# Inversion products of two heads as one 128x128 product, in a two-layer-plus-retention kernel

## The chip, the cores and the metric

The kernel runs on one core of one Trainium2 chip. The metric is the device time of one execution in microseconds (us). Of the kernel before, three runs gave 2006.71 us as their median (2004.17 to 2009.91). All rows are of one profiled execution of 2008.5 us.

## The reference

The model works on 512 tokens of width 1024: an RWKV-7 layer with its MLP, a sliding-window attention layer with its MLP, and a retention and Fourier block with a gated convolutional feed-forward. The part that matters here is the recurrence of the RWKV-7 layer, 16 heads of 64 channels, in float32:

```python
def wkv7(r, w, k, v, a, b):
    def step(S, inp):
        r_t, w_t, k_t, v_t, a_t, b_t = inp
        sa = jnp.einsum('bhvk,bhk->bhv', S, a_t)
        S = S * w_t[:, :, None, :] + sa[..., None] * b_t[:, :, None, :] + v_t[..., None] * k_t[:, :, None, :]
        y = jnp.einsum('bhvk,bhk->bhv', S, r_t)
        return S, y
```

The kernel computes it in chunks of 64 tokens. Inside a chunk the corrections `sa` of the 64 steps depend on each other through a strictly triangular 64x64 matrix per head; the kernel inverts identity minus that matrix.

## The kernel before, in words

**Layout.** Channels lie on the 128 partitions in 8 blocks (CB = 8), so a block holds two heads: head 0 on partitions 0 to 63, head 1 on 64 to 127. There are 8 chunks (NCH) of 64 tokens (HC), taken in 4 groups of two; x is the chunk within its group, g the group.

**The inversion.** It goes by five levels (LEVELS = 5). At each level the triangular matrix LL is masked so that only that level's blocks stay (LM, on GpSimd, `level_mask`, L2922), and two products follow: `inverse_left` (L2294) multiplies the masked matrix with the inverse so far, Z, which lies in the right half of the tile GBZ; ScalarE copies the result out of PSUM (QS, L914); `inverse_right` (L2302) multiplies the transposed inverse TI with QS; VectorE adds the result to Z (`inverse_sum`, L1474) and transposes Z for the next level (`turned`, L1468, one instruction over 128 partitions). Each product is made per block and per head: a 64x64 stationary matrix on 64 partitions, 64 moving columns, 8 blocks x 2 heads = 16 matmuls in the code. In float32 each becomes two weight loads and two matmuls in the profile, so 32 of each.

**The other products.** Score products feed the recurrence: `score_wide` (L2265, 128 moving columns; four blocks per job) and `score_narrow` (L2274 and L2276, 64 columns, eight blocks per job). They read one head's partitions and write the other head's (`cross`), so they use the two 64x64 quarters of the array that the inversion products of the same two heads don't. VectorE masks the wide ones (`score_mask`, L1460), ScalarE copies the narrow ones (L903). The recurrence itself is made of `correction` (L2381), `values_sum` (L2351), `output_states` (L2340), `solved` (L2363) and `off` (L2322 to L2331).

**The order.** It is written out by hand as beats. Beat b issues on TensorE: the left product of (g, level, x) = `inverse_at(b)` with the wide job of that beat between its matmuls; the right product of the beat before with the narrow job of this beat between its matmuls; then the recurrence's products for units of earlier beats; and in the first eight beats a `bonus` product (L2253, two matmuls of 512 columns on 32x128 tiles). A group has 10 beats (5 levels x 2 chunks), the four groups 40; about ten beats of recurrence alone follow. A table says which of the ten beats of a group have a wide job (8) and which a narrow one (8); the last group has fewer. Six score jobs run ahead of the first beat. Each engine has its own copy of the beat loop and waits on semaphores of the others: the left product for `lm` (GpSimd) and for the sum of its last level, the right one for QS and TI. LM has two tiles per x, so GpSimd may run two levels ahead. The stage is unrolled: each of its instructions is in the program once.

Of the kernel before, what the change touches and what calls it, by code (L numbers as in the profile page):

```python
# [16 lines left out]
ALU = mybir.AluOpType  # L17
# [3 lines left out]
P = 128  # L21
C = 1024
CB = C // P
# [14 lines left out]
LEVELS = 5  # L38
HC = 64
# [24 lines left out]
SQ_AT = {n: i for i, n in enumerate(SQUARES)}  # L64
# [115 lines left out]
def program(nc, t, out, book):  # L180
    ctx = ExitStack()
    with ctx:
# [3 lines left out]
        def at(name, kb, shape, dt=F32):  # L186
            return nc.alloc_sbuf_tensor_at(name, [P] + list(shape), dt, offset=base + int(kb * KB))
# [5 lines left out]
        sqs = at("sqs", 2, [N_SQ * P])  # L193
# [22 lines left out]
        PB = [ctx.enter_context(nc.psum_tensor(f"bank{i}", [P, 512], F32)) for i in range(8)]  # L216
# [4 lines left out]
        STEP = {}  # L221
# [31 lines left out]
        def phase_done(who):  # L253

            phases[who] += 1
            return 4 * phases[who]
# [105 lines left out]
        def masked_bank(beat):  # L362

            return (2, 7)[sorted(MASKED).index(beat % PER) % 2]
# [20 lines left out]
        GBZ = [at(f"GBZ{n}", kb, [CB, P]) for n, kb in enumerate((32, 40, 192, 196, 16, 24))]  # L385
        GKM = [at(f"GKM{n}", 20 + 8 * n, [CB, P]) for n in range(4)]
        LL = [at(f"LL{n}", 48 + 2 * n, [CB, HC]) for n in range(4)]
        VT = [at(f"VT{n}", 56 + 2 * n, [CB, HD]) for n in range(4)]
        LM = [[at(f"LM{x}{n}", 64 + 4 * x + 2 * n, [CB, HC]) for n in range(2)] for x in range(2)]
        QS = [at(f"QS{x}", 72 + 2 * x, [CB, HC]) for x in range(2)]  # L390
        TI = [at(f"TI{x}", 76 + 2 * x, [CB, HC]) for x in range(2)]
        SM = [at(f"SM{x}", 80 + 2 * x, [CB, HD]) for x in range(2)]
        WB = [at(f"WB{n}", 200 + 0.5 * n, [P]) for n in range(2)]
        DIAG = [at(f"DIAG{n}", 201 + 1.5 * n, [3 * P]) for n in range(2)]
# [132 lines left out]
        def half_of(name, n):  # L527

            return sq(name)[:, n * HC:(n + 1) * HC]

        def every(ap):

            return ap.unsqueeze(1).to_broadcast([P, CB, HC])

        def level(lv):

            return every(half_of(("lvl01", "lvl23", "lvl4id")[lv // 2], lv % 2))

        def pairs(ap):
            return ap.rearrange("p (a b) -> p a b", a=CB)  # L540
# [11 lines left out]
        def twice(ap):  # L552
            return ap.rearrange("p (a b) -> p a b", a=2)
# [25 lines left out]
        def tok(j):  # L579
            return slice(j * HC, (j + 1) * HC)  # L580

        def head(h):
            return slice(HD * h, HD * h + HD)
# [699 lines left out]
        def _(dve):  # L1283
# [92 lines left out]
            ds, di, dr, dg = (STEP["dve_" + n] for n in ("score", "inv", "rec", "gn"))  # L1376
# [68 lines left out]
            dve.tensor_copy(RKS[:], PB[4][:]).then_inc(dp.sem, dp.step())  # L1445
            dve.drain().then_inc(phase, 1)
            dve.wait_ge(phase, phase_done("dve"))
            dve.memset(SM[0][:], 0.0).then_inc(dr.sem, dr.step("m0"))
            ps, pi = STEP["pe_score"], STEP["pe_inv"]

            def bonus(cb):
# [10 lines left out]
            def turned(g, lv, x):  # L1462

                if lv == 0:
                    dve.wait_ge(STEP["pool_score"].sem, STEP["pool_score"].at(("z0", 2 * g + x)))
                else:
                    dve.wait_ge(di.sem, di.at(("z", g, lv - 1, x)))
                dve.transpose(TI[x][:], GBZ[(2 * g + x) % 6][:, :, HC:P]).then_inc(di.sem, di.step(("t", g, lv, x)))  # L1468

            def inverse_sum(g, lv, x):  # L1470

# [42 lines left out]
            for beat in range(BEATS):  # L1514
                z, m, w, y = inverse_at(beat - 1), job_at(MASKED, beat), recurrence_at(beat), recurrence_at(beat - 2)
# [6 lines left out]
                if z:  # L1522
                    g, lv, x = z
# [534 lines left out]
        def _(pe):  # L2058
# [51 lines left out]
            for kb in range(CB):  # L2110
                if kb == 4:
                    idle_work(6, PB[4])
                g = kb % 4
# [4 lines left out]
            for tb in range(TB):  # L2118
                mm = pe.matmul(PB[5][:, tb:tb + 1], PARTS[:, chunk(tb)], sq("ones")[:, 0:1], start=True, stop=True)
# [5 lines left out]
            for kb in range(CB):  # L2125
                pe.wait_ge(dl.sem, dl.at(("x", kb)))
                pe.matmul(PB[0][:], lg1[:, kb, 0:P], xl[kb][:], start=kb == 0, stop=kb == CB - 1)
                if kb % 4 == 3:
                    for g in range(4):
                        mm = pe.matmul(PB[1][32 * g:32 * g + 32, :], lg1[:, kb - 3 + g, P:LORA_G], xl[kb - 3 + g][:], start=kb == 3, stop=kb == CB - 1)  # L2130
# [4 lines left out]
            for kb in range(CB):  # L2135
                n = CB + 2 * kb
# [4 lines left out]
            for kb in range(CB):  # L2141
                pe.wait_ge(al.sem, al.at(("csq", kb)))
                g = kb % 4
# [15 lines left out]
            for q in range(3 * CB):  # L2159
                m, o = q % CB, PB[4 + q % 4][:]  # L2160
# [8 lines left out]
                if q < CB:  # L2169
# [3 lines left out]
                    mm = pe.matmul(o, low2["ga"][2][:, chunk(m)], hid2["ga"][1][:], start=False, stop=True)  # L2173
                elif q < 2 * CB:
                    mm = three(o, pieces(hid2["w"], chunk(m // 2)), pieces(low2["w"], slice(m % 2 * 512, m % 2 * 512 + 512)))
                else:
                    mm = three(o, pieces(low2["a"], chunk(m)), pieces(hid2["a"], every_token))
# [64 lines left out]
            din, ain, drc, arc = STEP["dve_inv"], STEP["act_inv"], STEP["dve_rec"], STEP["act_rec"]  # L2242
# [17 lines left out]
            def score_wide(j, job, bank, a):  # L2260

                cb = a + 4 * (job % 3)
                for h in range(2):
                    hs = head(h)
                    mm = pe.matmul(PB[bank][cross(h), chunk(a)], (BT if job < 2 else KT)[hs, cb, tok(j)], RA[hs, :, cb, tok(j)], start=True, stop=True)  # L2265
                if a == 3:
                    mm.then_inc(ps.sem, ps.step((j, job)))
# [21 lines left out]

            def inverse_left(g, lv, x, cb):  # L2290

                for h in range(2):
                    hs = head(h)
                    mm = pe.matmul(PB[x][hs, tok(cb)], LM[x][(LEVELS * g + lv) % 2][hs, cb, :], GBZ[(2 * g + x) % 6][hs, cb, HC:P], start=True, stop=True)  # L2294
                if cb == CB - 1:
                    mm.then_inc(pi.sem, pi.step(("q", g, lv, x)))

            def inverse_right(g, lv, x, cb):

                for h in range(2):  # L2300
                    hs = head(h)
                    mm = pe.matmul(PB[x][hs, tok(cb)], TI[x][hs, cb, :], QS[x][hs, cb, :], start=True, stop=True)  # L2302
                if cb == CB - 1:
                    mm.then_inc(pi.sem, pi.step(("z", g, lv, x)))

# [89 lines left out]
            for beat in range(BEATS):  # L2395
                q, z = inverse_at(beat), inverse_at(beat - 1)
                m, c = job_at(MASKED, beat), job_at(COPIED, beat)
                w, u, y, w2 = (recurrence_at(beat - ago) for ago in (0, 1, 2, -1))
                if q:
                    inverse_left_ready(*q)  # L2400
                if m:
                    score_free(MASKED, beat)
                for n in range(CB):
                    if q:
                        inverse_left(*q, n)
                    if m and n % 2 == 0:
                        score_wide(*m, masked_bank(beat), n // 2)
                if z:
                    pe.wait_ge(ain.sem, ain.at(("q", *z)))
                    pe.wait_ge(din.sem, din.at(("t", *z)))  # L2410
                if c:
                    score_free(COPIED, beat)
                for n in range(CB):
                    if z:
                        inverse_right(*z, n)
                    if c:
                        score_narrow(*c, 3, n)
                if y is not None:
                    off_ready(y)
                if w2 == 0:  # L2420
                    pe.wait_ge(dp.sem, dp.at(("bonus", CB - 1)))
                elif u is not None or w2 is not None:
                    pe.wait_ge(arc.sem, arc.at(("diag", beat - 1)))
                for n in range(CB):
                    if y is not None:
                        off(y, n)
                    if n in (0, 1) and w2 is not None:
                        mm = values_sum(w2, n)
                        if n == 1 and u is None:
                            mm.then_inc(pr.sem, pr.step(("diag", beat)))  # L2430
                    if n in (2, 3) and u is not None:
                        output_states(u, n - 2)
                    if n in (4, 6) and u is not None:
                        mm = solved(u, n // 2 - 2)
                        if n == 6:
                            mm.then_inc(pr.sem, pr.step(("diag", beat)))
                if w is not None:
                    correction(w)
                if beat < CB:
                    bonus(beat)  # L2440
                if beat == VSUM_AT:
                    early_sums()
# [401 lines left out]
            h = RH - 1  # L2844
# [45 lines left out]
        def _(pool):  # L2890
# [24 lines left out]
            def level_mask(g, lv, x):  # L2915

                j, at_level = 2 * g + x, LEVELS * g + lv
                if lv == 0:
                    pool.wait_ge(STEP["act_tok"].sem, STEP["act_tok"].at((j, 2)))
                if at_level >= 2:  # L2920
                    pool.wait_ge(STEP["pe_inv"].sem, STEP["pe_inv"].at(("q", (at_level - 2) // LEVELS, (at_level - 2) % LEVELS, x)))
                pool.tensor_tensor(LM[x][at_level % 2][:], LL[j % 4][:], level(lv), ALU.mult).then_inc(pc.sem, pc.step(("lm", j, lv)))  # L2922

            def scaled(j):

# [130 lines left out]
```

## Time and profile before

| what | value |
|---|---|
| median of 3 runs | 2006.71 us |
| profiled execution, its own time | 2008.5 us |
| its span, first to last instruction | 2006.6 us |
| TensorE busy | 1906.9 us (95%) |
| VectorE, ScalarE, GpSimd busy | 57%, 38%, 11% |
| the 40 beats with inversion products | 221.26 to 390.60 us |
| TensorE busy in them | 127.05 of 169.34 us |

A busy time is the union of an engine's records, so matmuls that overlap in different parts of the array count once. PE is TensorE's matmuls, PEld its weight loads, DVE VectorE, ACT ScalarE, POOL GpSimd. "Issue" is idle time for which the profile shows nothing that was waited for.

### The profile page before, as it was taken

The numbers are of one execution on the slowest core, as the hardware profiler recorded it, in microseconds if no ns is written. First come the engines' busy times: TensorE is split into PE (matmuls) and PEld (weight loads), VectorE is DVE, ScalarE is ACT, GpSimd is POOL, SyncE is SP. The second block draws the span as 40 slices with busy tenths as digits, with TensorE's granted clock in tenths as the row PEclk, the third lists the DMA queues.
The fourth block names the chain that finished last, engine by engine and source line by source line (L and its number), as shares of the span: only waits on it lengthen the run. The fifth ranks groups of instructions, "written<-read, shape, count | busy, mean of one in ns | idle before, by whom it ended". The sixth has DMA issues, their size and how long they took to land.

```text
span 2006.6 us, 34728 instructions
## 1 busy us (share of the span) xinstructions
PE 1906.9 (95%) x14308; PEld 1532.7 (76%) x14308; DVE 1139.9 (57%) x1749; ACT 771.7 (38%) x1255; POOL 221.6 (11%) x178
## 2 busy tenths in 40 slices
PE   7999966789999999998999999999999999999997
PEld 3877766667788787765778787877888788888885
DVE  6789755474444434567484746576554366566323
ACT  6777333334232212447532222235243244444211
POOL 1000344200201202014110202020000010000001
PEclk9999999999999999999999999999999989999999
DMA  5420000232332232220344454535520222322421
GB/s 196 139 84 32 3 4 4 84 131 95 93 96 92 77 114 79 98 69 33 126 147 159 148 180 143 208 126 169 156 77 32 74 84 90 110 94 84 152 89 42
DMA packets 61000, 201.44 MB, mean 100 GB/s; under 512 B 8000, under 2 KB 11200, under 8 KB 59584
## 3 DMA queue, kind: packets, MB, share of 16 engines
q1 hardware_dynamic: 60096, 192.93, 28.9%
q10 hardware_dynamic: 768, 6.55, 1.0%
q8 instruction: 103, 1.69, 0.4%
q14 instruction: 33, 0.27, 0.0%
HBM read 190.68 MB, written 6.42 MB: 98 GB/s over the span
## 4 chain that ended last, share of the span: by engine, by line
PE 70%; issue 19%; DVE 6%; POOL 2%; ACT 2%; DMA 0%; DVEq 0%; POOLq 0%; SPq 0%; ACTq 0%
PE bank L2097 17%; PE bank L2099 17%; PE bank L2098 17%; POOL HS L2958 2%; PE bank L2294 2%; PE bank L2302 1%; DVE HR L1682 1%; DVE wlo L1292 1%; PE bank L2265 1%; PE bank L2618 1%; PE bank L2604 1%; PE bank L2781 1%; DVE ADS L1668 1%; PE bank L2638 1%; PE bank L2104 1%
## 5 line engine op out<-in xcount | busy, mean ns | idle before, releaser
L1292 DVE TENSOR_TENSOR wlo<-raw,whi 128x1024 fp32r<-128x1024 f32 x270 | 327.4, 1223 | 568.9 <-ACT whi L741 567.7
L741 ACT ACTIVATE whi<-raw 128x1024 fp32r<-128x1024 f32 x270 | 282.2, 1057 | 708.5 <-PE bank L2099 691.9
L2097 PE MATMUL bank<-inh,whi 128*128 128x512 f32 x1200 | 470.8, 392 | 1.9 <-DVE inl L1559 1.6
L2099 PE MATMUL bank<-inh,wlo 128*128 128x512 f32 x1200 | 467.1, 389 | 0.0
L2098 PE MATMUL bank<-inl,whi 128*128 128x512 f32 x1200 | 467.0, 389 | 0.0
L2097 PEld LDWEIGHTS bank<-inh,whi 128*128 128x128 f32 x1200 | 225.3, 188 | 58.4 <-issue 6.6
L2099 PEld LDWEIGHTS bank<-inh,wlo 128*128 128x128 f32 x1200 | 225.2, 188 | 47.0
L2098 PEld LDWEIGHTS bank<-inl,whi 128*128 128x128 f32 x1200 | 225.3, 188 | 46.7 <-issue 0.7
L2097 PE MATMUL bank<-hidh,whi 128*128 128x512 f32 x576 | 228.6, 397 | 8.2 <-DVE HR L1682 5.4
L2099 PE MATMUL bank<-hidh,wlo 128*128 128x512 f32 x576 | 224.5, 390 | 0.0
L2098 PE MATMUL bank<-hidl,whi 128*128 128x512 f32 x576 | 224.3, 389 | 0.0
L2958 POOL TENSOR_TENSOR HS<-HR 128x512 f32<-128x512 f32 x64 | 85.8, 1374 | 678.1 <-DVE HR L1682 678.1
L2097 PEld LDWEIGHTS bank<-hidh,whi 128*128 128x128 f32 x576 | 108.1, 188 | 41.3 <-DVE HR L1682 14.7
L2099 PEld LDWEIGHTS bank<-hidh,wlo 128*128 128x128 f32 x576 | 108.1, 188 | 22.9
L2098 PEld LDWEIGHTS bank<-hidl,whi 128*128 128x128 f32 x576 | 108.2, 188 | 20.9
L2097 PE MATMUL bank<-xmh,whi 128*128 128x512 f32 x192 | 76.5, 398 | 0.0
L2098 PE MATMUL bank<-xml,whi 128*128 128x512 f32 x192 | 74.8, 389 | 0.0
L2099 PE MATMUL bank<-xmh,wlo 128*128 128x512 f32 x192 | 74.8, 389 | 0.0
L1668 DVE SCALAR_TENSOR_TENSOR ADS<-ADW,LT,ADS 128x1536 f32<-128x1536 f32 (+1 forms) x56 | 69.0, 1279 | 0.0
L2097 PE MATMUL bank<-GH,whi 128*128 128x512 f32 x176 | 68.6, 390 | 0.0
L2099 PE MATMUL bank<-GH,wlo 128*128 128x512 f32 x176 | 68.5, 389 | 0.0
L2098 PE MATMUL bank<-GL,whi 128*128 128x512 f32 x176 | 68.5, 389 | 0.0
(423 smaller groups left out, 2818.4 us busy)
## 6 DMA issues: line engine op xcount, KB each, us to landing
raw<-in_mlp_w SPq DMA_DIRECT2D x128, 512.0 KB, 3.6
ADW<-in_w_ada SPq DMA_DIRECT2D x32, 768.0 KB, 5.0
raw<-in_w_up SPq DMA_DIRECT2D x44, 512.0 KB, 3.5
raw<-in_w_in SPq DMA_DIRECT2D x28, 512.0 KB, 3.6
raw<-in_a_w_rkv SPq DMA_DIRECT2D x24, 512.0 KB, 3.4
raw<-in_w_down SPq DMA_DIRECT2D x22, 512.0 KB, 3.4
raw<-in_a_wo SPq DMA_DIRECT2D x8, 512.0 KB, 7.7
raw<-in_b_wq SPq DMA_DIRECT2D x8, 512.0 KB, 3.3
```

Source lines behind the costliest of these rows:

```text
L741: act.activation(whi[u % SLOTS][:, :], raw[u % SLOTS][:, :], ACT.Copy).then_inc(w_hi, 1)
L1292: dve.tensor_tensor(lo[:, :], r[:, :], h[:, :].bitcast(F32), ALU.subtract).then_inc(w_lo, 1)
L1668: dve.scalar_tensor_tensor(acc, w, c_, acc, ALU.mult, ALU.add).then_inc(dmo.sem, dmo.step(("sum", tag, v, k), ("sum", tag, k)))
L1682: dve.scalar_tensor_tensor(HR[m % 4][:], PB[m][:], 0.0, RS[:], ALU.max, ALU.mult).then_inc(dmlp.sem, dmlp.step(("r", nm, m)))
L2097: pe.matmul(o, w[:, wc], xh, start=start, stop=False)
L2098: pe.matmul(o, w[:, wc], xl_, start=False, stop=False)
L2099: return pe.matmul(o, r[:, wc], xh, start=False, stop=stop)
L2104: pe.matmul(o, xh, w[:, wc], start=start, stop=False)
L2265: mm = pe.matmul(PB[bank][cross(h), chunk(a)], (BT if job < 2 else KT)[hs, cb, tok(j)], RA[hs, :, cb, tok(j)], start=True, stop=True)
L2294: mm = pe.matmul(PB[x][hs, tok(cb)], LM[x][(LEVELS * g + lv) % 2][hs, cb, :], GBZ[(2 * g + x) % 6][hs, cb, HC:P], start=True, stop=True)
L2302: mm = pe.matmul(PB[x][hs, tok(cb)], TI[x][hs, cb, :], QS[x][hs, cb, :], start=True, stop=True)
L2958: pool.tensor_tensor(HS[m % 4][:], HR[m % 4][:], HR[m % 4][:], ALU.mult).then_inc(STEP["pool_mlp"].sem, STEP["pool_mlp"].step(("hs", nm, m)))
```

## The change

Both heads of a block go into one product. The stationary operands become 128x128 block-diagonal matrices, head 0's 64x64 matrix top left, head 1's bottom right, zero elsewhere: LM and TI get 128 columns per block. The level masks are laid out the same way in a new tile LVL (five levels x 128 columns), so that the mask product also writes LM's zeros: it reads LL twice over and writes 1024 elements per partition instead of 512. TI's zero halves are set once, and the transpose writes each head's diagonal block in an instruction of its own. The products' moving operands (Z and QS) and their results stay where they were. The wide and the narrow score jobs leave the loops of the inversion products and get loops of their own behind them.

```diff
-        LM = [[at(f"LM{x}{n}", 64 + 4 * x + 2 * n, [CB, HC]) for n in range(2)] for x in range(2)]
+        LM = [[at(f"LM{x}{n}", 64 + 20 * x + 4 * n, [CB, P]) for n in range(2)] for x in range(2)]
+        LVL = at("LVL", 204, [LEVELS, P])
-        TI = [at(f"TI{x}", 76 + 2 * x, [CB, HC]) for x in range(2)]
+        TI = [at(f"TI{x}", 76 + 16 * x, [CB, P]) for x in range(2)]
...
+            for x in range(2):
+                for h in range(2):
+                    dve.memset(TI[x][head(h), :, tok(1 - h)], 0.0).then_inc(dr.sem, dr.step(("zero", x)))
+            dve.memset(LVL[:], 0.0).then_inc(dr.sem, dr.step("zero levels"))
             dve.memset(SM[0][:], 0.0).then_inc(dr.sem, dr.step("m0"))
+            dve.wait_ge(dr.sem, dr.at("zero levels"))
+            for h in range(2):
+                masks = sqs[head(h), SQ_AT["lvl01"] * P:SQ_AT["lvl01"] * P + LEVELS * HC]
+                dve.tensor_copy(LVL[head(h), :, tok(h)], masks.rearrange("p (a b) -> p a b", a=LEVELS)).then_inc(dr.sem, dr.step("levels"))
...
-                dve.transpose(TI[x][:], GBZ[(2 * g + x) % 6][:, :, HC:P]).then_inc(di.sem, di.step(("t", g, lv, x)))
+                for h in range(2):
+                    dve.transpose(TI[x][head(h), :, tok(h)], GBZ[(2 * g + x) % 6][head(h), :, HC:P]).then_inc(di.sem, di.step(("t", g, lv, x)))
...
-                for h in range(2):
-                    hs = head(h)
-                    mm = pe.matmul(PB[x][hs, tok(cb)], LM[x][(LEVELS * g + lv) % 2][hs, cb, :], GBZ[(2 * g + x) % 6][hs, cb, HC:P], start=True, stop=True)
+                mm = pe.matmul(PB[x][:, tok(cb)], LM[x][(LEVELS * g + lv) % 2][:, cb, :], GBZ[(2 * g + x) % 6][:, cb, HC:P], start=True, stop=True)
...
-                for h in range(2):
-                    hs = head(h)
-                    mm = pe.matmul(PB[x][hs, tok(cb)], TI[x][hs, cb, :], QS[x][hs, cb, :], start=True, stop=True)
+                mm = pe.matmul(PB[x][:, tok(cb)], TI[x][:, cb, :], QS[x][:, cb, :], start=True, stop=True)
...
                 for n in range(CB):
                     if q:
                         inverse_left(*q, n)
-                    if m and n % 2 == 0:
-                        score_wide(*m, masked_bank(beat), n // 2)
+                for n in range(CB // 2):
+                    if m:
+                        score_wide(*m, masked_bank(beat), n)
...
                 for n in range(CB):
                     if z:
                         inverse_right(*z, n)
+                for n in range(CB):
                     if c:
                         score_narrow(*c, 3, n)
...
+                if at_level == x == 0:
+                    pool.wait_ge(STEP["dve_rec"].sem, STEP["dve_rec"].at("levels"))
...
-                pool.tensor_tensor(LM[x][at_level % 2][:], LL[j % 4][:], level(lv), ALU.mult).then_inc(pc.sem, pc.step(("lm", j, lv)))
+                pool.tensor_tensor(LM[x][at_level % 2][:].rearrange("p c (a b) -> p c a b", a=2), LL[j % 4][:].unsqueeze(2).to_broadcast([P, CB, 2, HC]),
+                                   twice(LVL[:, lv, :]).unsqueeze(1).to_broadcast([P, CB, 2, HC]), ALU.mult).then_inc(pc.sem, pc.step(("lm", j, lv)))
```

## Rows read from the trace of the kernel before

**Rows 1.** The page, TensorE's line: busy us (share of the span) xinstructions.

```profile
PE 1906.9 (95%) x14308; PEld 1532.7 (76%) x14308; DVE 1139.9 (57%) x1749; ACT 771.7 (38%) x1255; POOL 221.6 (11%) x178
```

**Rows 2.** Busy time by stretch, its columns in the first line.

```profile
core 0: us, PE busy (x) PEld busy (x) DVE busy (x) ACT busy (x) POOL busy (x), PEclk, DMA share, GB/s
221.26:390.60 169.34, 127.05 (x5539) 112.80 (x5536) 97.00 (x211) 55.43 (x107) 71.89 (x60) 1.00 0.02 4
225.00:247.00 22.00, 22.00 (x724) 16.05 (x718) 17.31 (x27) 7.16 (x12) 12.24 (x12) 1.00 0.01 4
264.81:268.39 3.58, 2.47 (x127) 2.33 (x127) 1.36 (x6) 0.60 (x1) 1.27 (x1) 1.00 0.02 5
```

**Rows 3.** Chain of waits, 221.26 to 390.60 us, shares by line.

```profile
by line: issue 24.0%; PE bank L2294 18.5%; PE bank L2302 17.2%; PE bank L2265 8.3%; PE bank L2276 6.0%; PE bank L2253 5.0%; PE bank L2331 2.6%; PE bank L2381 2.5%; PE bank L2324 2.3%; PE bank L2363 2.2%; PE bank L2329 2.1%; PE bank L2322 2.
```

**Rows 4.** TensorE's waits, same stretch: who waited for what, us, times, longest.

```profile
PE bank L2294 <- DVE GBZ L1474: 2.8, 4, 0.7
```

**Rows 5.** DMA queues, same stretch: packets, MB, share of 16 engines.

```profile
q8 instruction: 44, 0.72, 1.9%
```

**Rows 6.** Groups by line, 218 to 400 us: busy us, mean ns | idle before.

```profile
L2294 PE MATMUL bank<-GBZ,LM 64*64 64x64 f32 x1280 | 50.0, 222 | 12.8 <-issue 8.8 <-DVE GBZ L1474 2.8 <-POOL LM L2922 0.8
L2302 PE MATMUL bank<-QS,TI 64*64 64x64 f32 x1280 | 47.3, 219 | 4.8 <-issue 4.6
```

**Rows 7.** Timeline of TensorE ahead of the first beat: start us, us, instruction.

```profile
218.57 1.92 PE L2265 MATMUL bank<-RA,AA 64*64 64x128 f32 x32
220.32 1.10 PE L2274 MATMUL bank<-AA,RA 64*64 64x64 f32 x32
221.26 0.27 PE L2294 MATMUL bank<-GBZ,LM 64*64 64x64 f32 x2
```

**Rows 8.** Timeline of TensorE over the fifth beat.

```profile
233.47 0.27 PE L2294 MATMUL bank<-GBZ,LM 64*64 64x64 f32 x2
...
234.40 0.22 PE L2276 MATMUL bank<-sqs,AA 64*64 64x64 f32 x2
...
235.32 0.22 PE L2302 MATMUL bank<-QS,TI 64*64 64x64 f32 x2
235.48 1.12 PE L2253 MATMUL bank<-RKS,heads 32*128 32x512 f32 x2
236.53 0.27 PE L2294 MATMUL bank<-GBZ,LM 64*64 64x64 f32 x2
```

**Rows 9.** Timeline of weight loads: two unbroken runs of 128x128 products elsewhere.

```profile
1399.61 3.65 PEld L2695 LDWEIGHTS bank<-VC,KW 128*128 128x128 f32 x32 [0.91 <-ACT VC L1134]
...
1606.43 0.97 PEld L2840 LDWEIGHTS bank<-sqs,PARTS 128*128 128x128 f32 x8 [1.66 <-DVE MX L1995]
```

**Rows 10.** Groups by line and shape, weight loads.

```profile
L2294 PEld LDWEIGHTS bank<-GBZ,LM 64*64 64x64 f32 x1280 | 42.9, 134 | 23.5 <-issue 16.8 <-POOL LM L2922 5.6 <-POOL RA L2929 0.8
...
L2695 PEld LDWEIGHTS bank<-VC,KW 128*128 128x128 f32 x32 | 3.6, 192 | 0.9 <-ACT VC L1134 0.9
```

**Rows 11.** Groups by line and shape, VectorE and GpSimd.

```profile
L1468 DVE STREAM_TRANSPOSE TI<-GBZ 128x512 f32<-128x512 f32 x40 | 28.4, 710 | 1.1
...
L1310 DVE MEMSET hid<- 64x512 f32 x1 | 0.5, 485 | 0.0
L1448 DVE MEMSET SM<- 128x512 f32 x1 | 0.5, 485 | 0.3 <-DVEq L1446 0.3
...
L2922 POOL TENSOR_TENSOR LM<-LL,sqs 128x512 f32<-128x512 f32 x40 | 50.3, 1274 | 28.6 <-PE bank L2294 28.6
L2929 POOL TENSOR_TENSOR RA<-RA,FS 128x512 f32<-128x512 f32 x14 | 14.5, 1058 | 32.3 <-DVE GKM L1460 32.3
...
L2903 POOL TENSOR_TENSOR lw_lo<-lw,lw_hi 128x1024 fp32r<-128x1024 f32 x1 | 2.4, 2425 | 14.9 <-DVE gb_xh L1335 14.9
```

**Rows 12.** Timeline of VectorE and GpSimd at the start of the stage.

```profile
216.98 0.69 DVE L1460 TENSOR_TENSOR GBZ<-bank,sqs 128x512 f32<-128x512 f32 x1 [0.48 <-PE bank L2265]
...
218.71 1.26 POOL L2913 TENSOR_TENSOR GBZ<-GBZ,sqs 128x512 f32<-128x512 f32 x1 [167.12 <-DVE GBZ L1460]
219.94 1.27 POOL L2922 TENSOR_TENSOR LM<-LL,sqs 128x512 f32<-128x512 f32 x1
```

More of the change, by code:

```diff
@@ L533, in every @@
             return ap.unsqueeze(1).to_broadcast([P, CB, HC])
-        def level(lv):
-            return every(half_of(("lvl01", "lvl23", "lvl4id")[lv // 2], lv % 2))
         def pairs(ap):
@@ L2410, in _ @@
                     pe.wait_ge(din.sem, din.at(("t", *z)))
+                    if z[:2] == (0, 0):
+                        pe.wait_ge(drc.sem, drc.at(("zero", z[2])))
                 if c:
```

## The prediction

> **What bounds the kernel now.** Four views, in this order. The page first: TensorE is busy for 95% of the span [rows 1], so what a stage costs on TensorE goes straight into the time, unless TensorE idles there. The change touches one stage only, the chunked recurrence, whose 40 beats with an inversion product run from 221.26 to 390.60 us. The table by stretch [rows 2] says that TensorE does idle there: 127.05 us busy of 169.34, with the granted clock at 1.00 (the 2.4 GHz level). The chain of waits of the same stretch [rows 3] says for what: 24.0% of it, 40.6 us, is "issue", time in which TensorE waits for no other engine; the waits for others are small (the largest, for the sum of VectorE, is 2.8 us, [rows 4]). The DMA view names it [rows 5]: the instruction queue fetched 44 times in that stretch, 0.72 MB, so 16 KB each. At 64 bytes an instruction (my reading of 16 KB against the 5539 matmuls and 5536 weight loads of [rows 2]: 11075/44 = 252) that is one fetch per block of some 254 matmuls and loads, and one fetch every 169.34/44 = 3.85 us. The third line of [rows 2] is one such block: 127 + 127 instructions, 3.58 us, 2.47 of it busy.
>
> Is 3.85 us a floor for a block, or a pause added to each? From 225 to 247 us [rows 2] TensorE runs 1442 of them in 22.00 us without idling, 3.9 us for 254: work that takes as long as the fetch shows no pause. So I read a floor. A block costs the larger of 3.85 us and its own work; today's work is 127.05/44 = 2.9 us.
>
> **The change, part by part.** (All terms are us, against the profiled execution, 2008.5 us with a span of 2006.6; the median shown is 2006.7, 1.8 below it.)
>
> 1. *Instructions removed.* Each product had 32 matmuls and 32 loads (16 products of 64x64, each in two instructions), 1280 + 1280 matmuls over 40 products of each kind [rows 6]. They become 16 + 16 each. 2560 of 11075 instructions go, so 33.8 fetches stay: the floor falls from 169 to 130.
>
> 2. *What a product costs.* Today 32 matmuls take 0.93 (L2294 from 233.47 until L2276 starts at 234.40, [rows 8]), 29 ns each. That is the rate of two tiles, rows 0-63 to columns 0-63 and rows 64-127 to 64-127, working side by side. The new ones take the whole array. A load of 128 columns instead of 64 has a record of 192 ns instead of 134 [rows 10], and in unbroken runs 128x128 instructions in f32 follow each other at (3.65 - 0.19)/31 = 0.112 with 128 moving columns and at (0.97 - 0.19)/7 = 0.111 with one [rows 9]. Our 64 moving columns lie between these, so 0.112: 16 x 0.112 = 1.79 a product. Added: 1.79 - 0.93 = 0.86, over 80 products 68.8. Nothing hides it: from 225 to 247 TensorE is busy all the time, and later each block has only the fetch pause as cover, which is counted in step 5. Bounds from the rows: 0.058, one tile's pace today (two tiles at 29 ns), which adds 0; and 0.192, the load's whole record with no overlap, which adds 80 x (3.07 - 0.93) = 171. The runs of [rows 9] have the new shape, so I take theirs and give the ends little.
>
> 3. *The covered products come out.* Score products write "across" (rows of one head to the columns of the other), so they used the two tiles that the inversion left free. The beat at 233.47 shows it [rows 8]: left product and 16 wide matmuls together end by 234.40, right product and 32 narrow ones together by 235.35. Alone, 32 wide ones take 220.32 - 218.57 = 1.75 and 32 narrow ones 221.26 - 220.32 = 0.94 [rows 7]. A whole-array matmul leaves no tile free, and the change puts both kinds in loops of their own. Wide jobs in these beats: 28 (8 a group in three groups, 4 in the last), each 16 matmuls, 0.875: 24.5, less the 0.05 by which they stretched the left section: 23.1. Narrow jobs: 30 at 0.94: 28.2. Together 51.3. Bounds: 0 if they still overlapped something, which the whole array excludes but for the edges; 51.3 is at the upper end.
>
> 4. *Changing tiles.* Before L2253, which uses 32x128 tiles, the next start, 235.48, comes 0.14 after the last L2302 (a pair at 235.32 and 235.34) instead of 0.03: 0.11 to 0.12 extra; behind it L2294 starts at 236.53, when two of 0.53 are through, so nothing [rows 8]. Two entries a beat into 128x128: 80 x 0.12 = 9.6. Bounds: 0, and 0.22 (one matmul's own record, [rows 6]) at each of 160 changes, 35.
> The Trainium skill ("TensorEngine Tiling (Array Packing)", Key Properties) says that changing the tiling mode, not just the tile, drains the engine. The change makes four mode changes a beat where the later beats now have none. By the rule every one of the 160 would cost a drain, and the rows show one side of a pair only; the time that it gives is rival B below.
>
> 5. *The pauses go.* Work after: 127.05 + 68.8 + 51.3 + 9.6 = 256.8 over 33.8 blocks is 7.6 a block, twice the floor of 3.85. A block spans about one beat and always holds some 30 whole-array matmuls (3.6 alone), so no block falls under the floor. All 42.3 of idle time but the 1.7 that is no issue goes: 258.5 against 169.3, +89.2.
>
> 6. *VectorE.* The transpose [rows 11] is now one per head, on 64 partitions. A memset of 64x512 takes 485 ns, as much as one of 128x512, so halving partitions saves nothing: 40 more of 0.71 (0.64 apart), 28 in all. They come behind the sum for which the next left product waits, and the right product that reads them comes a beat later, so beats of 6 cover them; in today's beats it would be up to 26. Cost 0.
>
> 7. *GpSimd.* A mask product doubles to 1024 elements: from 1.27 to about 2.42, as the 128x1024 row shows [rows 11]. Ten beats hold 10 of these, two additions of 1.26 and four scalings of 1.06: 31. The ten beats take 10 x 6.5 = 65. Hidden; its cover ends at beats of 3.1.
>
> 8. *Start.* VectorE zeroes four half tiles (4 x 0.485) and the level tile (0.6, scaled from the same row) and copies the levels twice (each taken as nearly one memset of [rows 11], 0.9 together) before its first score mask: 3.5, of which 0.5 was idle there [rows 12]. GpSimd's first addition then starts 3.0 later and its first level mask [rows 12] takes 1.15 longer; the first left product waits for just these: +4. Bounds 2 and 5.
>
> Sum: 89.2 + 4 = 93. 2008.5 + 93 = 2101.5 for a profiled execution, 2100 as a median.
>
> **The rivals.**
> A, *the other side: supply of instructions decides.* If a 128x128 product took no longer than a 64x64 pair and the score products still ran beside it, work would stay at 127 under the new floor of 130: 130 - 169 + 4 = -35, 1972. For it: the 24% of [rows 3] and one fetch per 3.85. Against: the 0.112 of [rows 9]. It decides from the point where the work after stays below 169 - 4 = 165; already the uncovered scores alone (127 + 51 = 178) pass that, so both steps 2 and 3 must be wrong. 0.04.
> B, *each of the 160 changes of mode drains,* 0.22 each: 35 instead of 9.6, 2125. For it: the 0.12 of [rows 8] is for one side only, and small matmuls keep little in flight. Against: 64x64 after 32x128 cost nothing. 0.13.
> C, *the pause is added to every block.* Then 40.6/44 = 0.92 stays for each of 33.8 blocks, 31 more: 2131. Against: no idle time from 225 to 247. 0.08.
> D, *the work overlaps more than counted:* half of the 51.3 of step 3 stays covered, because loads of one mode slip under the matmuls of the other: 2074. Nothing in the rows shows it. 0.07.
> E, no change of more than 0.3% (6 us, about what a measurement of this kernel can tell from none): work would have to end at 165 by chance. 0.01.
>
> **The numbers.** Forecast 2100, chance 0.67, its own range 2085 to 2115 (the bounds of steps 2 and 8 and small waits). The range reaches over D and over B and C: 2068 to 2134; A and the far tails stay out, below 0.2. Slower by over 0.3%: 0.95; the same: 0.01; faster: 0.04.
>
> **What would show it.** In the profile after: L2294 and L2302's successors with 640 records each, 112 ns from start to start, 1.8 us a product (steps 1, 2); wide and narrow matmuls behind them, not between (step 3); a beat like the one at 233.47 at about 3.06 + 0.86 x 2 + 0.83 + 0.94 + 0.24 = 6.8; the stage some 259 long with "issue" near nothing and 33 or 34 fetches (step 5); GpSimd's mask at 2.4, and nobody waiting for it behind the first. All other stages as before. I am wrong if the 128x128 products follow each other at 60 ns or less, if TensorE still idles for a sixth of the stage (C), or if gaps of 0.2 stand at each change of mode (B).

## The result, and the profile after

The changed kernel takes 2130.93 us as a median of four runs (2101.66 to 2160.65) against 2006.66; the ratio is 1.057, with an interval of 1.046 to 1.068. The ratio leaves out the longest run, whose clock was lowest, and takes the mean of the other three; the medians alone give 1.062. On the two chips of e1 and e12 the ratio was 1.049 (1.041 to 1.057) and 1.064 (1.059 to 1.069). It is slower, as forecast. The profiled execution, 2101.66 us with a span of 2099.7, lies on the forecast for one (2101.5); the median lies 31 above 2100, near the upper end of the range (2134). Two questions, then: where 93 us come from in the profiled run, and why most runs take some 30 or 60 more.

The table by stretch: the stage of the 40 beats, then its first ten beats and the other thirty, after the change.

```profile
core 0: us, PE busy (x) PEld busy (x) DVE busy (x) ACT busy (x) POOL busy (x), PEclk, DMA share, GB/s
225.98:481.45 255.47, 255.47 (x4252) 237.32 (x4254) 127.45 (x249) 54.98 (x106) 113.95 (x60) 0.99 0.01 3
225.98:290.61 64.63, 64.63 (x712) 55.37 (x712) 30.18 (x44) 10.15 (x17) 29.84 (x16) 0.95 0.01 2
290.61:481.45 190.84, 190.84 (x3546) 181.95 (x3542) 97.28 (x206) 44.82 (x89) 84.11 (x45) 1.00 0.02 4
```

And the same two parts of the kernel before:

```profile
221.26:252.34 31.08, 29.45 (x1022) 22.32 (x1019) 23.56 (x36) 11.44 (x20) 17.95 (x15) 1.00 0.02 4
252.34:390.60 138.26, 97.59 (x4517) 90.48 (x4518) 73.45 (x176) 43.99 (x88) 53.93 (x46) 1.00 0.02 5
```

The stage went from 169.34 [rows 2] to 255.47 us, and TensorE, idle for a quarter of it before, is never idle now: 255.47 busy of 255.47, with a quarter fewer matmuls (4252 instead of 5539). The first ten beats grew by 33.5, the others by 52.6, the start came 4.7 later (225.98 instead of 221.26): 90.8 of the span's 93.1. The rest, 2.3, is outside the stage.

The chain of waits of the stage; "issue", 24.0% in [rows 3], is no longer among the first lines, and both products together are 60% instead of 36%.

```profile
by line: PE bank L2298 30.7%; PE bank L2304 29.5%; PE bank L2271 11.5%; PE bank L2282 10.0%; PE bank L2259 3.4%; PE bank L2280 2.5%; PE bank L2324 2.3%; PE bank L2383 2.1%; PE bank L2333 2.0%; PE bank L2331 2.0%; PE bank L2326 1.5%; PE bank
```

The DMA view, instruction fetches of the stage, 34 where [rows 5] has 44:

```profile
q8 instruction: 34, 0.56, 0.9%
```

The timeline of TensorE over the fifth beat, the one of [rows 8] (start us, us, instruction):

```profile
252.85 2.00 PE L2298 MATMUL bank<-GBZ,LM 128*128 128x64 f32 x16
254.78 1.09 PE L2271 MATMUL bank<-RA,AA 64*64 64x128 f32 x16
255.80 2.00 PE L2304 MATMUL bank<-QS,TI 128*128 128x64 f32 x16
257.73 1.15 PE L2282 MATMUL bank<-sqs,AA 64*64 64x64 f32 x32
258.81 1.12 PE L2259 MATMUL bank<-RKS,heads 32*128 32x512 f32 x2
259.86 0.32 PE L2298 MATMUL bank<-GBZ,LM 128*128 128x64 f32 x1
```

From start to start: left product (L2298) 1.93, wide job (L2271) 1.02, right product (L2304) 1.93, narrow job (L2282) 1.08, bonus (L2259) 1.05; in all 7.01 where it was 3.06. Before, the first two together took 0.93 and the next two 0.95.

### The profile page after: what moved, and what is told of

It is laid out like the page before. It is cut to its first block, busy times and chain, and to the rows that moved or that the text cites. A ratio compares the mean times of both kernels' runs of the same rounds, so it can differ in the third digit from the quotient of the medians.

```text
span 2099.7 us, 32217 instructions
## 1 busy us (share of the span) xinstructions
PE 2038.6 (97%) x13028; PEld 1658.8 (79%) x13028; DVE 1174.6 (56%) x1796; ACT 771.9 (37%) x1255; POOL 264.8 (13%) x178
## 4 chain that ended last, share of the span: by engine, by line
PE 73%; issue 16%; DVE 6%; POOL 2%; ACT 2%; DMA 0%; DVEq 0%; POOLq 0%; SPq 0%; ACTq 0%
PE bank L2103 17%; PE bank L2105 16%; PE bank L2104 16%; PE bank L2298 4%; PE bank L2304 4%; POOL HS L2967 2%; PE bank L2271 2%; PE bank L2282 1%; DVE HR L1688 1%; PE bank L2098 1%; PE bank L2624 1%; DVE wlo L1289 1%; PE bank L2610 1%; PE bank L2787 1%; DVE ADS L1674 1%
## 5 line engine op out<-in xcount | busy, mean ns | idle before, releaser
L2930 POOL TENSOR_TENSOR LM<-LL,LVL 128x1024 f32<-128x1024 f32 x40 | 93.6, 2354 | 37.8 <-PE bank L2298 37.8
L2298 PEld LDWEIGHTS bank<-GBZ,LM 128*128 128x128 f32 x640 | 75.5, 194 | 12.8 <-POOL LM L2930 5.4
L2298 PE MATMUL bank<-GBZ,LM 128*128 128x64 f32 x640 | 81.0, 280 | 4.3 <-POOL LM L2930 4.3
L2304 PE MATMUL bank<-QS,TI 128*128 128x64 f32 x640 | 79.4, 277 | 0.0
L2304 PEld LDWEIGHTS bank<-QS,TI 128*128 128x128 f32 x640 | 74.5, 192 | 4.7 <-issue 4.6
```

The lines of the kernel that those rows point to most:

```text
L2298: mm = pe.matmul(PB[x][:, tok(cb)], LM[x][(LEVELS * g + lv) % 2][:, cb, :], GBZ[(2 * g + x) % 6][:, cb, HC:P], start=True, stop=True)
L2304: mm = pe.matmul(PB[x][:, tok(cb)], TI[x][:, cb, :], QS[x][:, cb, :], start=True, stop=True)
L2930: pool.tensor_tensor(LM[x][at_level % 2][:].rearrange("p c (a b) -> p c a b", a=2), LL[j % 4][:].unsqueeze(2).to_broadcast([P, CB, 2, HC]) ...
```

## The experiments

Most change one thing of one of the two kernels; times are medians, and each time of the kernel before was taken on the same chip. Spans and beats are of the profiled runs. Estimates "by the line of spans and clocks" use 0.44 us of span for each us at half clock, a fit through the 14 runs of the changed kernel in the result, e1 and e12; the time at half clock is 2 x (1 - mean clock) x span.

**e1, the changed kernel again**, no edit.

> The changed kernel once more, to see its times beside their granted clocks, since its runs lay between 2101.66 and 2160.65 us while the profiled one gave 2101.66. Theory (work of TensorE, plus a clock that falls in some runs): times again spread over some tens of us, and each run's span follows from its clock: the four spans so far rise by 28.1, 59.0 and 30.5 us while the time at half clock, 2 x (1 - clock) x span, rises from 50 to 111, 177 and 119, so half a microsecond for each at 1.2 GHz. Rival (waits that fall differently from run to run, not the clock): spans that differ at one and the same clock.

2115.47 (2100.2 to 2132.3) against 2012.74. Its spans and mean clocks were 2098.2 at 0.990, 2103.3 at 0.986, 2123.8 at 0.975 and 2130.3 at 0.972, near the line that was expected (these four give 0.42 us for each us at half clock, the first four 0.46): the spread is the clock's. What the clock does, and where, e8 and e12 show.

**e2, the order alone.** In the kernel before:

```diff
                 for n in range(CB):
                     if q:
                         inverse_left(*q, n)
-                    if m and n % 2 == 0:
-                        score_wide(*m, masked_bank(beat), n // 2)
+                for n in range(CB // 2):
+                    if m:
+                        score_wide(*m, masked_bank(beat), n)
...
                     if z:
                         inverse_right(*z, n)
+                for n in range(CB):
                     if c:
                         score_narrow(*c, 3, n)
```

> The kernel before, with one thing of the change: wide and narrow score jobs come behind the inversion products in loops of their own; the products stay 64x64 per head. Step 3 of the prediction: work of the 40 beats rises from 127 by 51 to 178, while the instructions, so the floor of 3.85 us a fetch, stay (169). A late beat with everything has some 300 instructions (4.6 us by the floor) and 4.8 us of work, an early one is work alone (3.06 + 0.83 + 0.94): early ten beats +15, late ones +2 to +10. I expect 2020 to 2035 us. Rival (the supply of instructions alone decides): no change, 2007. Rival (a pause is added to every block whatever its work): +51, 2058.

2017.53 against 2012.74, ratio 1.0017 (1.0005 to 1.0029): 5 us where 13 to 28 were expected (2020 to 2035 on a kernel before of 2007). Work rose by 27.0 (37.03 + 117.04 against 127.05), not by the 51 counted. By stretch, first ten beats and the other thirty:

```profile
221.85:259.00 37.15, 37.03 (x1022) 30.18 (x1017) 23.26 (x36) 10.77 (x18) 17.53 (x15) 1.00 0.02 4
259.00:396.07 137.07, 117.04 (x4524) 111.77 (x4526) 73.57 (x176) 44.73 (x89) 54.42 (x46) 1.00 0.02 5
```

The thirty later beats hold 19.5 us more work (117.04 against 97.59) and take 1.2 less: the pauses are not added to the work but take it in, as the floor of the prediction has it, and "issue" falls from 24.0% to 11.6% of the stage's chain. The stage again had 44 fetches; that these are what sets the floor is read from their count and from "issue", and this run, which leaves their number alone, can't show it. The early beats, where little idled before (29.45 busy of 31.08), pay: +6.1. That is less than the 15 expected, because two jobs in different quarters of the array still overlap at their borders. The first wide matmuls start here before the last left ones, and the right product starts at 238.24, before the last wide ones (238.56), so this wide job adds some 0.3 to its beat and not 0.83:

```profile
236.97 0.97 PE L2294 MATMUL bank<-GBZ,LM 64*64 64x64 f32 x26
237.74 0.33 PE L2265 MATMUL bank<-RA,AA 64*64 64x128 f32 x2
237.78 0.28 PE L2294 MATMUL bank<-GBZ,LM 64*64 64x64 f32 x4
```

**e3, whole-array products with the score jobs between them**: the changed kernel with e2's edit taken back.

> The changed kernel with the score jobs back between the matmuls of the inversion products, as before. In the changed kernel's trace a change between whole-array and quarter matmuls costs 0.10 to 0.14 us from start to start. Here a beat with a wide job makes 8 such changes in its left part and one with a narrow job 16 in its right part. Theory (each change drains): 28 x 6 x 0.12 + 30 x 14 x 0.12 = +70 us over the changed kernel's 2102, so some 2170. Rival D of the prediction (loads of one mode slip under matmuls of the other, so covering would come back if the order were restored): 2050 to 2075.

2343.24, 1.16 of the kernel before, far over both theories. Its clock, 0.904 over the whole profiled run, is the larger part of it:

```profile
227.10:237.00 9.90, 9.86 (x66) 7.23 (x66) 2.01 (x3) 1.19 (x2) 9.90 (x5) 0.50 0.01 2
260.00:300.00 40.00, 40.00 (x187) 28.80 (x188) 9.74 (x14) 2.98 (x5) 8.26 (x4) 0.50 0.00 0
300.00:730.00 430.00, 428.77 (x3890) 344.73 (x3891) 111.53 (x226) 49.57 (x97) 92.87 (x50) 0.62 0.01 3
```

TensorE is busy nearly throughout, and most of the time at 1.2 GHz. An estimate parts the two: a mean clock of 0.904 over 2352.2 us makes 451 us at half clock, 401 more than in the changed kernel, which by the line of spans and clocks cost 177. Without them the span would be some 2176, 76 more than the changed kernel's, where the theory of costly changes had 70. So the old order would not have saved the score jobs' cover; with their separate 1.02 and 1.08 in the beat above, rival D is out.

**e4, everything but TensorE's part.** The changed kernel, score jobs between the products again, and the products per head on the diagonal halves:

```diff
-                mm = pe.matmul(PB[x][:, tok(cb)], TI[x][:, cb, :], QS[x][:, cb, :], start=True, stop=True)
+                for h in range(2):
+                    hs = head(h)
+                    mm = pe.matmul(PB[x][hs, tok(cb)], TI[x][hs, cb, tok(h)], QS[x][hs, cb, :], start=True, stop=True)
...
```

> Everything of the change but TensorE's part: GpSimd builds 128-column masks (2.35 us instead of 1.27), VectorE transposes per head and fills the tiles at the start, while TensorE keeps the 64x64 products with the score jobs between them, reading the diagonal halves. Steps 6 to 8: covered but for the start, +4: 2010 to 2013 us. Rival (VectorE or GpSimd becomes the bound once beats are short, as they are here at 4.1 us: ten masks and the rest take GpSimd 30 of 41): up to +26, 2033, with waits of TensorE for LM or GBZ.

2018.97 against 2012.74, +6.2 (ratio 1.0030, 1.0016 to 1.0043). In the profiled run the first left product comes 3.6 later (224.9 instead of 221.3), and the stage is 3.3 longer, 172.7. Of the wait for GpSimd's masks, 4.3 is that late start and only 3.0 lies in later beats:

```profile
PE bank L2300 <- POOL LM L2932: 7.3, 4, 4.3
```

What lengthens the stage is the clock of its first two beats, which end at 234.87 and take 9.96 where they took 6.08. The clock falls in the pause before the first product:

```profile
224.90:234.00 9.10, 9.10 (x195) 7.41 (x196) 3.46 (x6) 1.80 (x4) 9.10 (x5) 0.53 0.02 4
```

**e5 and e6, instructions that bring no work**, in either kernel:

```diff
                 if q:
+                    for _ in range(32):
+                        pe.wait_ge(in_tri, 16)
                     inverse_left_ready(*q)
```

> The kernel before with 32 more waits on TensorE at the head of each of the 40 beats, all on a semaphore that has long had its value: instructions that bring no work. Theory of a floor (3.85 us for a block of 256 instructions): 1280 more are 5 fetches, so +19 us in the late beats and in the early ones alike (these run just at the floor): 2028 to 2034 against the kernel before. Rival (TensorE's work and its waits for other engines bound the stage, fetches are incidental): within 4 us of the kernel before.

> The changed kernel with the same 32 waits a beat. Theory of a floor: a beat has some 230 instructions in 6.4 us, 262 with the waits, 3.9 us by the floor, so no change: 0 to +3 us against the changed kernel, stage 255 to 258. Rival (each instruction, or each fetch, costs its own time whatever the work): +19 here as well.

e5: 2031.29 against 2009.17, as the floor had it, but not for its reason: 46 fetches, not 49, and 20.5 us of waits for VectorE's transposes. e6: 2224.86, where 0 to 3 us over the changed kernel were expected. TensorE idled 32 of the stage's 365.6 us, at the heads of the beats:

```profile
PE bank L2298 <- issue: 19.0, 21, 1.4
PE bank L2298 <- POOL LM L2932: 9.7, 5, 4.6
PE bank L2298 <- DVE TI L1474: 7.4, 7, 1.4
```

The waits take time of their own, so this pair can't test the floor; I don't count it for it. What e6 did show is the clock: 0.70 from 300 to 592 us, while the kernel before idles more (42 us of 169) and stays at 1.00. By the line of spans and clocks that is 81 of its 112 us over the changed kernel (an estimate, from a mean clock of 0.947). The waits alone, with 64x64 products, take e5's stage to 0.94.

**e7, one of the two products.** Left products whole-array, wide jobs behind them; right products per head with the narrow jobs between, as in e4.

> Half of the change: left products whole-array with the wide jobs behind them, right products 64x64 per head with the narrow jobs between them. By the durations of the changed kernel (16 x 0.115 = 1.84 a product, wide jobs alone 0.88, 0.12 for each of two changes of mode a beat): work 127 + 40 x 0.9 + 23 + 10 = 196 against a floor of 150, so stage 196 to 202, +27 to +33, and +4 to +5 at the start: 2042 to 2052. If the whole-array products cost by a state of the engine that both kinds together bring about (the clock in the first place), this one keeps its clock and its runs lie within 5 us; if single whole-array runs are enough, its runs spread like the changed kernel's.

2036.46 against 2009.17: +27, below the 2042 to 2052 expected. The stage takes 188.8 where 196 to 202 were counted, 183.4 of it busy, "issue" 2.0% of its chain; its right products start before the wide job ahead of them has issued its last matmul (237.70 and 238.02 in the second beat), an overlap that was not counted. The first product uses up most of the 42 us of pause, so it costs 27 with its start; the second one then pays in full, some 65 more. The four runs lie between 2030.4 and 2040.7, clock 0.984 to 0.988: a spread of 10 us and not 5, but none on the lower levels, so in these four runs whole-array left products alone did not bring the long fall.

**e8, the fillings off the path**: GpSimd zeroes and fills LVL before its first addition, VectorE zeroes TI's halves among its first score masks and behind its first transpose.

> The changed kernel with the filling of the tiles off the path: GpSimd, idle until its first addition, zeroes and fills the level tile; VectorE zeroes the halves of TI in its gaps between the first score masks. The changed kernel started its first left product at 226.0 instead of 221.3 and ran that beat at half clock behind the pause (8.1 us for work of some 5.1). Theory: -4.5 for the start, less the 1.1 that the first mask costs more, and -3 if the clock does not fall: 5 to 7 us under the changed kernel (2092 to 2095 for a run of full clock). Rival (the fall of the clock has nothing to do with the pause): -3.5.

The first left product starts at 221.85, 4.1 earlier, and the first beat takes 4.93 instead of 8.09: for this the theory held. Yet the median is 2125.99, far over the 2092 to 2095 expected of a run of full clock, because its four runs all lost the clock for longer (means of 0.969 to 0.977); with that taken off by the line of spans and clocks, the profiled span of 2122.6 would be some 2096 (an estimate). This profile shows the loss. Busy time by stretch:

```profile
240.00:260.00 20.00, 20.00 (x210) 16.91 (x209) 10.90 (x17) 2.98 (x5) 8.27 (x4) 0.99 0.00 1
260.00:280.00 20.00, 20.00 (x137) 17.52 (x137) 6.01 (x9) 2.22 (x4) 4.38 (x3) 0.50 0.01 2
280.00:300.00 20.00, 20.00 (x124) 17.42 (x122) 4.17 (x6) 1.96 (x4) 1.08 (x1) 0.50 0.00 1
300.00:320.00 20.00, 20.00 (x174) 18.96 (x175) 5.01 (x8) 2.73 (x6) 10.72 (x6) 0.50 0.00 1
320.00:340.00 20.00, 20.00 (x330) 18.92 (x327) 9.18 (x19) 3.31 (x7) 7.86 (x5) 0.80 0.01 2
340.00:360.00 20.00, 20.00 (x393) 19.12 (x392) 10.71 (x25) 4.97 (x10) 5.94 (x3) 1.00 0.01 3
```

From about 260 to 328 us the granted clock is 0.50 (1.2 GHz), with TensorE busy in every microsecond from 240 on. It falls in the seventh beat, and it is back in the thirteenth.

**e9 and e11, an added product of 512 columns.** The changed kernel with one more product ahead of each left one:

```diff
+                if q:
+                    pe.matmul(PB[q[2]][:], sq("ones"), V[:, 0, :], start=True, stop=True)
                 for n in range(CB):
                     if q:
                         inverse_left(*q, n)
```

> The changed kernel with one more product ahead of each of the 40 left ones, 128x128 against 512 columns into the same bank, overwritten by the left product: two instructions of some 0.43 us in which the array streams columns without a load between. It adds 0.86 x 40 = 34 us of work. Theory (the clock falls because whole-array products of 64 columns spend half their time on loads, so the array does little though it is never idle): with the columns the clock stays at its upper level, all runs lie within 10 us of each other, near 2100 + 34 = 2134, clock 0.986 or more, and perhaps 3 lower since the first beat is not at half clock. Rival (the clock falls by the mode changes or by chance of the chip, whatever else streams): runs spread by 30 us and more as the changed kernel's did, 2134 to 2190.

> The kernel with the 512-column products ahead of the left ones once more, on the same chip as the changed kernel, for the clocks of more runs. So far one run in five had a mean clock under 0.98, of the changed kernel five in eight. Theory (streaming columns hold the clock): at most one or two of some six runs under 0.98, the rest at 2133 to 2139. Rival (it falls by chance whatever streams): three or more under 0.98.

e9: 2133.2, 2134.2, 2137.4, 2138.9, and one of 2195.9, where all five were expected within 10 us. e11, its profiled run among five: 2136.3 to 2139.0, clock 0.987 or 0.988. So 9 of 10 runs kept the clock and lie within 6 us, at the price of the added work.

**e12, the changed kernel beside e11.**

> The changed kernel once more beside it: more than half of its runs under a mean clock of 0.98, the spans again on the line of 0.47 us for each us at half clock: 2100 at 0.99 to 2160 at 0.96. Rival (the fall belongs to a chip or an hour, not to the kernel): as few as in the other kernel, or none.

2132.11 (2129.9 to 2164.9), all six under 0.98, and the profiled one shows the fall at the same place:

```profile
260.00:265.00 5.00, 5.00 (x44) 3.94 (x44) 2.36 (x4) 0.60 (x1) 2.35 (x1) 1.00 0.00 0
265.00:270.00 5.00, 5.00 (x26) 5.00 (x25) 1.12 (x2) 0.60 (x1) 0.00 (x0) 0.50 0.01 3
325.00:330.00 5.00, 5.00 (x32) 4.62 (x28) 0.69 (x1) 0.27 (x1) 4.14 (x3) 0.50 0.00 0
330.00:335.00 5.00, 5.00 (x81) 4.79 (x80) 2.39 (x4) 0.98 (x2) 0.00 (x0) 0.67 0.01 3
335.00:340.00 5.00, 5.00 (x104) 4.65 (x103) 2.52 (x4) 1.09 (x2) 2.35 (x1) 1.00 0.00 0
```

Its stage takes 286.6 instead of 255.5. All 14 runs of the changed kernel fall into three groups:

| runs | span, us | mean clock |
|---|---|---|
| 3 | 2098.2 to 2103.3 | 0.986 to 0.990 |
| 8 | 2123.8 to 2130.4 | 0.971 to 0.975 |
| 3 | 2158.2 to 2162.9 | 0.956 to 0.959 |

Steps of 30 us, as one and as two such stretches at half clock would give; of the third group there is no profile. The clock fell for 68 us in either profile, 265 to 333 here. Under 0.98 are 11 of 14 runs here and all 4 of e8, 1 of 10 with the added product (e9, e11), none of 4 of e7, and none of 10 of e2, which has this order with 64x64 products.

**e10, whole-array products only where nothing runs beside them**: 10 left and 9 right products in the later beats, on the kernel before; fillings as in e8.

```diff
+        def alone(beat, table):
+            return beat > PER and not job_at(table, beat)
...
-                        inverse_left(*q, n)
+                        inverse_left(*q, n, alone(beat, MASKED))
...
-                        inverse_right(*z, n)
+                        inverse_right(*z, n, alone(beat, COPIED))
```

> The kernel before, with whole-array products only where they have no score job beside them and the fetches bound TensorE: 10 left and 9 right products after the first ten beats. The other 61 stay 64x64 with the score jobs between; only the masks of the 10 are 128 wide on GpSimd; transposes are per head in all; the fillings stand in gaps as in the start experiment. 19 x 32 = 608 instructions less, 2.4 fetches, -9 us by the floor; the 19 products add 0.9 and two changes of mode of 0.12 each, 1.1 us, where a block has 0.95 us of pause. Theory: the two nearly balance, between -6 and 0: 2001 to 2009 on a kernel before of 2007 to 2009. Rival (supply decides all): -9. Rival (work decides all): +21.

2016.20 against 2009.45, ratio 1.0044 (1.0025 to 1.0062), worse than expected. The fetches fell from 44 to 42 and work rose by 18; over the same 40 beats, which start 1.5 earlier here:

```profile
219.79:388.78 168.99, 145.34 (x5234) 131.66 (x5231) 127.96 (x253) 55.33 (x107) 82.60 (x60) 0.99 0.02 6
```

The stage is as long as before (168.99 against 169.34): what two fetches fewer may give, the added work takes. The profiled run is the fastest of the seven, 2009.92. The others have clocks of 0.981 to 0.987 where most runs of the kernel before have 0.988 to 0.992, and by the line of spans and clocks that is some 5 of the 6.7 us between the medians (an estimate); no profile shows where those runs lose it. So no version here beats the kernel before.

## Why the prediction was right, and where it was short

**Steps 1 and 5, fetches and pauses: right.** 33.8 fetches counted, 34 made; issue gone; the stage 255.5 against 258.5. e2 shows that today's later beats are held by a floor and not by pauses added to work. That the fetches make it stays an inference: e5 and e6, which were to test it, could not. Rival C is out by the 255.47 of 255.47 busy. Its number, 2131, is the median's, and shows that a time alone can pick the wrong cause.

**Step 2, the product: right.** The 16 loads of a left product have a record of 1.86 in all, so (1.86 - 0.19)/15 = 0.111 apart:

```profile
252.85 1.86 PEld L2298 LDWEIGHTS bank<-GBZ,LM 128*128 128x128 f32 x16 [0.76 <-issue]
```

The matmuls start 0.112 apart too, all but the first two of a product, which are 0.160 apart. That makes 1.83 where 1.79 was counted, and of 1.93 to the next job the remaining 0.10 is the change of tiles behind it.

**Step 3, the cover of the score jobs: right for this change, wrong as a term by itself.** Alone the jobs cost 1.02 and 1.08 in the beat above. But e2 shows that their order by itself brings 27 us of work, not 51, and 5 of time; with 64x64 products about half of the cover stays at the borders, and it is the whole-array products that take this half too.

**Step 4, changes of tiles: too small.** These are single starts in the trace. From the last start of a product to the next 64x64 job it is 0.205 instead of 0.112, and from a 64x64 job to a product 0.148 to 0.199, not the 0.03 to 0.10 of the job's own pace; behind either border the first two starts are 0.05 further apart than the rest. So a border costs some 0.14 on both sides of a product, not only at the entry. The stage has some 127 such borders (12 left products have no wide job behind them), which makes 18 us where 9.6 were counted and rival B had 35. The border from the narrow job to the bonus, 0.14 in the beat above, was there before, and the one from the bonus back to the left product shows only the wider first gap. The Trainium skill's rule ("TensorEngine Tiling (Array Packing)", Key Properties), that a change of mode drains the engine, fits the borders between 64x64 and 128x128, at some 0.14 each and not at the 0.22 of rival B; whether the time is a drain the trace does not tell. That the stage still came out 3 shorter than forecast has one visible reason: the 127.05 busy of before counts at each pause the tail of a record of 0.22, where the next start would come 0.03 later. With 48 pauses in the trace these are 9 us of work that never was (an estimate). I have argued this, not shown it. With the 8 of the borders and 3 of the clock (below) on the other side, some 5 us stay without a place.

**Steps 6 to 8.** VectorE's transposes were covered. The masks took 2.35:

```profile
L2930 POOL TENSOR_TENSOR LM<-LL,LVL 128x1024 f32<-128x1024 f32 x40 | 93.6, 2354 | 37.8 <-PE bank L2298 37.8
```

The start was 4.7 late, for 4 forecast. e4, all of it without TensorE's part, costs 6.2. Left out was the clock of the first beat, 0.58 behind the pause at the start: 8.09 us, where e8's takes 4.93 at full clock. That is 3 us. Both first beats, the changed kernel's and e8's:

```profile
225.98:234.07 8.09, 8.09 (x66) 6.90 (x66) 2.01 (x3) 1.19 (x2) 8.09 (x5) 0.58 0.01 2
221.85:226.78 4.93, 4.93 (x67) 4.04 (x67) 3.02 (x6) 1.19 (x2) 4.93 (x3) 1.00 0.01 3
```

**What failed: the step from a profiled run to the median.** "2100 as a median" took the clock of the stage for given, 1.00 in [rows 2]. The whole-array products change it: in eight runs of fourteen the time is 30 us longer, and in the one of them that was profiled these are six beats at half clock; three more runs have twice that. No step of mine asked for it. The own range 2085 to 2115 missed the median for this; the wide one held it, and that is luck: it reached so far on account of rivals B and C, and neither made the 31 us.

**What stays open.** Why some runs lose the clock once, some twice and some not at all. That the added product of 512 columns holds it is shown by counts (1 in 10 against 11 in 14) and with one kind of addition only; it also makes each beat some 0.85 us longer, and no run has longer beats without the columns. That the early beats are the place rests on two profiles. How much of e3's time is the clock and how much the 22 more changes of mode in a full beat is an estimate; no run parts them. That the floor of the later beats is the instruction fetch is not tested by itself.

## What to carry to other kernels

Two 64x64 products on opposite quarters of the array cost here half of one 128x128 product made of the same two (0.93 against 1.83 for 8 blocks), and leave the other quarters to whoever works across: fusing them halved the instructions and doubled the time of TensorE. Before counting removed instructions as gain, compare the new work of a stretch with the floor seen in the trace (here 3.85 us for one fetch of about 256 instructions). Such a trade can pay only where work lies well below it, and none here did: e7 and e10 show how soon the room is used up. Look at the granted clock of the new mixture too, over several runs and not in one profile.

## What the runs showed of the hardware

TensorE's clock fell to its lower level in a stretch in which it was never idle (20.00 busy of 20.00 at 0.50 in e8), whereas the kernel before idles a quarter of the time and holds the upper level (1.00 in [rows 2]). The Trainium skill ("TensorE: Matmul & The Clock Gate", Why this matters for your kernels) advises to keep TensorE continuously busy to have the upper level. In these runs continuous busy records did not assure it: what TensorE did when the clock fell was whole-array products of 64 columns, each behind a load of 0.111, with the score jobs between them.
